# Norms around the two layers of a hybrid decoder step: five tiles in a pipeline instead of one after the other, and the first projection step by halves of the tokens

## Chip, cores and metric

The kernel runs on one core of a Trainium2 chip. The metric is the device time of one execution in microseconds (us), the median of several runs. PE is TensorE, DVE VectorE, ACT ScalarE, POOL GpSimd and SP SyncE, which issues most of the loads. A matmul record's first size is its stationary operand, its second the moving one.

## The reference

```python
for layer in range(2):
    hp, hs = rms_norm(y_prompt, norm_pre), rms_norm(y_sample, norm_pre)
    # layer 0: differential attention over a paged cache; layer 1: retention with a recurrent state
    o = mixer(hp @ w_in, hs @ w_in)            # gate from the same projection
    y = y + rms_norm(o @ w_out, norm_post)

def rms_norm(x, w):
    return x * lax.rsqrt(mean(x * x, axis=-1) + 1e-6) * w
```

There are 512 prompt tokens and 64 sample tokens (T = 576) of 2048 features, all in float32. Before a layer x is normed with weight `norm_pre`; behind it the layer's output y is normed with weight `norm_post` and added to x.

## The kernel before

Projections keep features on the partitions and tokens on the free axis: `XH` and `XL` hold the normed x in two parts (high and low), `WH` and `WL` a weight chunk in two parts. A weight chunk is 512 rows by 256 columns (512 KB), loaded by SP into one of two slots of `WR`, and split by ACT (`WH`, a copy) and DVE (`WL`, a subtraction): stage `split_w`. A step of the projection makes 256 output columns for all 576 tokens: in the input projections it goes over 4 chunks, 32 tiles, and each tile is 6 matmuls, 3 products (high-high, high-low, low-high) for each of two halves of 288 tokens. `Projections.tile` gives out the tiles one by one; behind the third tile of chunk n it puts the split of chunk n+1 and the load of chunk n+3. The attention and retention work is set between the tiles by hand written slot numbers (`attention_pair`, `layer_one`), and the one list of stages that results is run by every engine in order, each engine doing its own part of a stage and waiting on counted semaphores.

The norms need tokens on the partitions. They work on five tiles of tokens (four of 128 and one of 64), and stand in `norm_segment(stage)`, called for stage 0 (before layer 0), 1 (between the layers) and 2 (at the end). The list alternates `y_tile` and `x_tile`:

- `y_tile` (stages 1 and 2): PE transposes a tile of y into the four `low_banks`; ACT squares all 2048 features from there and sums them; DVE scales the sum (L1303), POOL raises it to -0.5 (L1644), DVE multiplies by that and by `wpost` (L1605), and then adds the tile of x that was loaded (L1609).
- `x_tile` (stages 0 and 1): ACT squares the tile of x (L1266), DVE and POOL make the factor as above, ACT multiplies the tile by it, PE transposes it into the four `high_banks`, ACT copies 16 pieces times `wpre` to `XH`, and DVE subtracts to `XL` (L1620).

x and the scaled tile have two buffers each. SP loads a tile of x when its buffer is free. In the last parts of the output projections PE's sums are added to y by DVE (L1346, L1347), two additions for each 128 output columns.

## Time and profile before

| what | us |
|---|---|
| median of 3 runs | 4121.02 (4120.16 to 4127.6) |
| the profiled execution | 4107.18 |
| its span, first to last instruction | 4105.4 |
| first projection matmul, layer 0 | 90.37 |
| last matmul of layer 0, first of layer 1 | 1980.8, 2087.71 |
| last projection matmul of all | 4053.4 |

The time outside the span is 1.8 us. Mean granted clock of TensorE over the span is 0.965 of full speed. The span falls into two long stretches of projections with the mixers' work among them, and three short ones for the norms: before 90.37, from 1980.8 to 2087.71, and behind 4053.4.

### The profile page before, as it was taken

The page shows a single profiled execution, that of the slowest core. Times are in us where ns is not written, and L with a number is a line of the kernel's source. Part 1 is how long each engine was busy: PE and PEld are TensorE (multiplying, and loading weights), DVE is VectorE, ACT ScalarE, POOL GpSimd, SP SyncE. Part 2 cuts the span into 40 slices and gives each one's busy share as a digit, 9 for nine tenths or more (in the row PEclk, how much of TensorE's full clock was granted, in tenths as well). Part 3 has the DMA queues.
Part 4 walks back from the last instruction along what each step waited for, and adds up shares of the span by engine and source line. Part 5 has one row for each costly group of instructions (what it writes and reads, how often), then busy time and mean ns, then how long its engine had stood idle before and what let it go on. Part 6 is the DMA issues. An engine that isn't in the chain of part 4 may idle for free.

```text
span 4105.4 us, 69674 instructions
## 1 busy us (share of the span) xinstructions
PE 3767.5 (92%) x26880; PEld 3289.5 (80%) x26880; DVE 1427.7 (35%) x2278; ACT 1138.2 (28%) x1905; POOL 125.1 (3%) x76
## 2 busy tenths in 40 slices
PE   2998999999999998999579999999999999989996
PEld 2987777777777776776579989898988888879996
DVE  2234333333343334333432423233333334233333
ACT  4233223322332333231332222222222222222221
POOL 0000000200020002002000000000000000000000
PEclk7999999999999998999789999999999999999998
DMA  2355777677767775764323334343424243343323
GB/s 75 106 173 164 233 214 236 190 232 221 238 191 235 218 231 182 228 191 147 113 73 112 125 117 134 111 145 95 154 80 157 79 153 104 133 140 116 106 83 129
DMA packets 466203, 632.41 MB, mean 154 GB/s; under 512 B 39441, under 2 KB 288914, under 8 KB 462738
## 3 DMA queue, kind: packets, MB, share of 16 engines
q1 hardware_dynamic: 401538, 555.71, 43.4%
q10 hardware_dynamic: 64336, 72.24, 5.1%
q8 instruction: 216, 3.54, 0.4%
q14 instruction: 113, 0.93, 0.1%
HBM read 555.61 MB, written 70.65 MB: 153 GB/s over the span
## 4 chain that ended last, share of the span: by engine, by line
PE 53%; DVE 3%; ACT 2%; issue 2%; ACTq 2%; DMA 1%; POOL 1%; SPq 1%; DVEq 0%; POOLq 0%
PE low_banks L832 42%; PE high_banks L832 7%; PE high_banks L835 3%; POOL area L1644 1%; DVE area L1583 1%; ACTq L1245 1%; DVE WL L1328 1%; ACT XH L1055 1%; DVE area L1605 1%; DMA area<-in_cache_v 0%; ACTq L1215 0%; ACT WH L1055 0%; ACTq L1214 0%; PE low_banks L835 0%; ACT area L1055 0%
## 5 line engine op out<-in xcount | busy, mean ns | idle before, releaser
L832 PE MATMUL low_banks<-XH,WH 128*128 128x288 f32 x6656 | 1527.0, 311 | 46.2 <-DVE XL L1333 16.3
L832 PE MATMUL low_banks<-XH,WL 128*128 128x288 f32 x6656 | 1431.9, 297 | 0.0
L832 PE MATMUL low_banks<-XL,WH 128*128 128x288 f32 x6656 | 1428.8, 296 | 0.0
L832 PEld LDWEIGHTS low_banks<-XH,WH 128*128 128x128 f32 x6656 | 1072.5, 191 | 197.0 <-issue 154.5
L832 PEld LDWEIGHTS low_banks<-XH,WL 128*128 128x128 f32 x6656 | 1077.4, 190 | 0.0
L832 PEld LDWEIGHTS low_banks<-XL,WH 128*128 128x128 f32 x6656 | 1077.3, 190 | 0.0
L1328 DVE TENSOR_TENSOR WL<-WR,WH 128x1024 fp32r<-128x1024 f32 x416 | 509.3, 1224 | 965.2 <-ACT WH L1055 964.1
L1055 ACT ACTIVATE WH<-WR 128x1024 fp32r<-128x1024 f32 x416 | 439.9, 1057 | 981.4 <-PE low_banks L832 672.7
L832 PE MATMUL high_banks<-area 128*32 128x512 f32 (+7 forms) x3696 | 670.2, 553 | 45.2 <-issue 17.0
L835 PE MATMUL high_banks<-eye_sb,area 128*128 128x128 f32 (+2 forms) x3048 | 458.8, 287 | 203.2 <-ACT area L1055 150.1
L835 PEld LDWEIGHTS high_banks<-eye_sb,area 128*128 128x128 f32 (+2 forms) x3048 | 362.7, 147 | 346.4 <-issue 182.2
L1055 ACT ACTIVATE area<-high_banks 128x512 f32<-128x512 f32 x480 | 271.9, 569 | 1231.8 <-PE high_banks L835 807.3
L832 PEld LDWEIGHTS high_banks<-area 128*32 128x32 f32 (+4 forms) x3696 | 233.7, 147 | 225.9 <-issue 181.0
L1411 DVE COPY area<-high_banks 128x512 f32<-128x512 f32 x256 | 176.9, 691 | 601.6 <-PE high_banks L835 562.7
L1644 POOL TENSOR_TENSOR area<-area,power 128x1 f32<-128x1 f32 (+2 forms) x72 | 124.9, 1735 | 3970.4 <-DVE area L1303 3970.4
L1112 ACT ACTIVATE area<-low_banks 128x288 f32<-128x288 f32 x192 | 79.0, 411 | 377.8 <-PE low_banks L832 356.6
L1583 DVE SCALAR_TENSOR_TENSOR area<-area,high_banks 128x512 f32<-128x512 f32 x128 | 87.2, 745 | 51.1 <-PE high_banks L832 51.0
L1564 DVE SCALAR_TENSOR_TENSOR area<-area,high_banks 128x512 f32<-128x512 f32 x48 | 35.8, 747 | 166.5 <-PE high_banks L832 164.7
L1346 DVE TENSOR_TENSOR area<-low_banks,area 128x288 f32<-128x288 f32 x80 | 36.6, 458 | 161.0 <-PE low_banks L832 161.0
L1113 ACT ACTIVATE area<-low_banks 128x288 f32<-128x288 f32 x192 | 79.1, 412 | 6.0
L1620 DVE SCALAR_TENSOR_TENSOR XL<-high_banks,wpre,XH 128x128 fp32r<-128x128 f32 (+1 forms) x160 | 40.4, 329 | 72.9 <-ACT XH L1055 72.9
L1596 DVE TENSOR_TENSOR area<-high_banks,area 128x512 f32<-128x512 f32 (+1 forms) x40 | 25.6, 641 | 112.1 <-PE high_banks L835 112.1
(93 smaller groups left out, 901.1 us busy)
## 6 DMA issues: line engine op xcount, KB each, us to landing
area<-in_cache_k SPq DMA_DIRECT2D x512, 256.0 KB, 4.1
area<-in_cache_v SPq DMA_DIRECT2D x512, 256.0 KB, 3.9
WR<-in_w_in_ret SPq DMA_DIRECT2D x192, 512.0 KB, 3.6
WR<-in_w_in_attn SPq DMA_DIRECT2D x128, 512.0 KB, 5.2
out<-area ACTq DMA_DIRECT2D x73, 512.0 KB, 3.9
area<-in_state_ret SPq DMA_DIRECT2D x64, 512.0 KB, 5.5
WR<-in_w_out_ret SPq DMA_DIRECT2D x64, 512.0 KB, 3.4
WR<-in_w_out_attn SPq DMA_DIRECT2D x32, 512.0 KB, 4.9
```

Of the source, the lines that this page charges most:

```text
L832: return nc.tensor.matmul(out, a, b, start=start, stop=stop, skip_group_check=True)
L835: return nc.tensor.matmul(out, a, ident[0:n, 0:n], start=True, stop=True, is_transpose=True, skip_group_check=True)
L1055: return nc.scalar.activation(out, in_, ACT.Copy, scale=scale)
L1112: o.link(nc.scalar.activation(dst[:, 0:HALF], bank[2 * cb][:, 0:HALF], f))
L1113: last = nc.scalar.activation(dst[:, HALF:T], bank[2 * cb + 1][:, 0:HALF], f)
L1245: act.dma_start(st_out[g + b * HEADS], Sin[:, b, :].rearrange("p (e v) -> p e v", e=2)).then_inc(sem["state_out"], 16)
L1328: v.tensor_tensor(WL[:, slot, :, :], WR[:, slot, :, :], WH[:, slot, :, :].bitcast(f32), SUB).then_inc(sem["w_lo"], 1)
L1411: v.tensor_copy(KTs[u % 2][:, :, pp * 128:(pp + 1) * 128], bank[5][:, :].rearrange("p (j s) -> p j s", j=4)).then_inc(sem["drained5"], 1)
L1583: v.scalar_tensor_tensor(out=mine, in0=mine, scalar=hc[:, 388:389], in1=bank[4 + j][:, :], op0=MUL, op1=ADD).then_inc(sem[f"drained{4 + j} ...
L1605: v.scalar_tensor_tensor(out=yv, in0=low[0:R, :, :].rearrange("p a b -> p (a b)"), scalar=n[:, 1:2], in1=wpost[0:R, :], op0=MUL, op1=MUL). ...
L1620: last = v.scalar_tensor_tensor(out=XL[:, j, xc], in0=bank[4 + j // 4][:, (j % 4) * 128:(j % 4) * 128 + R], scalar=wpre[:, stage, j:j + 1] ...
L1644: nc.gpsimd.tensor_tensor(out, a, power[0:R, 0:n], ALU.pow).then_inc(sem[name], 1)
```

## The change

`norm_segment` gives way to `norm_before`, `norm_between` and `norm_last`, which are built by the class `Norm` from smaller stages, and several tiles are under way at once.

- y's squares are no longer summed from the transposed tile. Behind each step of the last part of an output projection ACT squares the 2 x 576 finished values (`y_sq`), and DVE adds them to `yacc` (8 steps for each layer). One group of matmuls with a column of ones then sums over the features for all five tiles (`y_rstd`), and POOL makes all factors in two instructions.
- y's tile comes from PE by ordinary matmuls with a diagonal matrix that holds `norm_post` (`post_diag`), not by transposes; DVE multiplies by the factor and adds x in one pass, in two halves. At the end of the kernel the tiles take the two halves of PSUM in turn.
- x's five tiles have a buffer each. Between the layers and at the end they are loaded, with the row of weights, beside the last part of the output projection. `norm_pre` is now multiplied with tokens on the partitions: tiles 0 and 4 get factor and weights in one pass on DVE; tiles 1 and 3 (and between the layers also 2) get the weights on POOL (`x_weigh`) and the factor on ACT. Copies to `XH` and subtractions to `XL` go by bank (4 of 512 columns).
- The first step of both input projections goes by halves of the tokens: all four chunks for tokens 0 to 287, and the four chunks again, loaded and split a second time, for tokens 288 to 575. Its first half starts when tiles 0 to 2 are there; the transposes of tile 3 stand behind its 10th tile, those of tile 4 behind its 26th.
- At the start SP loads x before the small constants; the exponentials of lambda are made later. The wait before the shared area changes hands (`relay_area`) no longer holds projections and weight loads, which now stand ahead of it.

```diff
 
-    def step(self, w, cols, rows, kts, **kinds):
+    def step(self, w, cols, rows, kts, by_half=False, **kinds):
+        half_chunks = len(rows)
+        if by_half:
+            rows, kts = rows + rows, kts + kts
         count = len(rows) * 2 * CH
         for i in range(count):
...
-                                                     new_x=i == 0, start=chunk == 0 and k == 0, stop=chunk == len(rows) - 1 and k == CH - 1,
+                                                     new_x=i == 0 or by_half and i == count // 2, halves=(chunk // half_chunks,) if by_half else (0, 1),
+                                                     start=chunk % half_chunks == 0 and k == 0, stop=(chunk + 1) % half_chunks == 0 and k == CH - 1,
                                                      full=full)))
...
+    loads = norm_loads(1)
     for n in range(64):
         out += proj.tile()
+        if n % 8 == 3 and loads:
+            out.append(loads.pop(0))
+        if n % 8 == 2 and n > 8:
+            out.append(Stage("y_sq", s=n // 8 - 1))
+    assert not loads
+    out.append(Stage("y_sq", s=7))
     return out
...
+class Norm:
+
+    def __init__(self, stage):
+        self.stage = stage
+        self.y, self.sq, self.weighed, self.scaled, self.tr = {}, {}, {}, {}, {}
+
+    def load(self, t):
+        return [Stage("load_x_tile", t=t, stage=self.stage)]
+
+    def sum_y(self, t):
+        wide = self.stage == 2 and t % 2
+        freed = self.y.get(t - 2 if self.stage == 2 else t - 1)
+        self.y[t] = Stage("y_tr", t=t, stage=self.stage, wide=wide, freed=freed)
+        return [self.y[t]]
+
+    def store(self, t):
+        return [Stage("store_x", t=t, stage=self.stage, after=self.y[t])]
+
+    def square(self, t):
+        self.sq[t] = Stage("x_sq", t=t, stage=self.stage, after=self.y.get(t))
+        return [self.sq[t]]
+
+    def weigh(self, t):
+        self.weighed[t] = Stage("x_weigh", t=t, after=self.y.get(t), freed=self.tr.get(t - 2))
+        return [self.weighed[t]]
+
+    def scale(self, t):
+        weighed = self.weighed.get(t)
+        self.scaled[t] = Stage("x_scale", t=t, by="act" if weighed else "dve", after=self.sq[t], weighed=weighed, freed=self.tr.get(t - 2))
+        return [self.scaled[t]]
+
+    def transpose(self, t):
+        in_low = self.stage == 0 and t == 1
+        freed = [x for u, x in self.tr.items() if not x.a["in_low"]]
+        self.tr[t] = Stage("x_tr", t=t, in_low=in_low, after=self.scaled[t], freed=freed[-1] if freed and not in_low else None)
+        return [self.tr[t]]
+
+    def close(self, proj):
+        out = []
+        for n in range(32):
+            if n == 10:
+                out += self.transpose(3) + self.scale(4)
+            if n == 26:
+                out += self.transpose(4)
+            out += proj.tile()
+        return out
+
+
+def norm_before(proj):
+
+    n = Norm(0)
+    out = n.load(0) + [Stage("load_norm", stage=0)] + n.load(1) + n.load(2) + proj.load(0) + proj.load(1) + n.load(3) + n.load(4)
+    out += [Stage("load_consts")]
+    out += n.square(0) + n.square(1) + n.weigh(1) + n.scale(0) + n.square(2) + n.transpose(0) + n.scale(1) + [Stage("split_w", slot=0)]
+    out += proj.load(2) + n.scale(2) + n.square(3) + n.transpose(1) + n.weigh(3) + n.square(4) + n.transpose(2) + n.scale(3)
+    out += [Stage("lambda_dot")]
+    return out + n.close(proj) + [Stage("lambda_exp")]
+
+
+def norm_between(proj):
+
+    n = Norm(1)
+    out = [Stage("y_rstd")]
+    out += n.sum_y(0) + n.square(0) + n.sum_y(1) + n.weigh(1) + n.scale(0) + n.square(1) + n.store(0)
+    out += n.sum_y(2) + n.transpose(0) + n.weigh(2) + n.square(2) + n.scale(1) + n.store(1)
+    out += n.sum_y(3) + n.transpose(1) + n.weigh(3) + n.square(3) + n.scale(2) + n.store(2)
+    out += n.sum_y(4) + n.transpose(2) + n.square(4) + n.scale(3) + n.store(3) + n.store(4)
+    return out + n.close(proj)
+
+
+def norm_last():
+
+    n = Norm(2)
+    out = [Stage("y_rstd")]
+    for t in range(5):
+        out += n.sum_y(t) + n.store(t)
     return out
+
+
+def norm_loads(stage):
+    out = [Stage("load_x_tile", t=t, stage=stage) for t in range(5)]
+    return [out[0], out[1]] + ([Stage("load_norm", stage=stage)] if stage < 2 else []) + out[2:] + [Stage("post_scale", stage=stage)]
 
 
...
-            proj.step("in0", "qkvg".index(kind) * D + (2 * pair + hh) * 256, rows, xs, kind=kind, hh=hh)
+            proj.step("in0", "qkvg".index(kind) * D + (2 * pair + hh) * 256, rows, xs, by_half=pair == hh == 0 and kind == "q", kind=kind, hh=hh)
...
-            proj.step("in1", col, rows, xs, kind=["q", "k", "v", "v", "g", "g"][s] + "r", hh=s % 2)
+            proj.step("in1", col, rows, xs, by_half=h == s == 0, kind=["q", "k", "v", "v", "g", "g"][s] + "r", hh=s % 2)
...
-                    for half in range(2):
+                    for half in halves:
...
-            def y_tile(g, t, stage):
-                R = TILES[t][1]
-                for n in ("proj0_drained", "proj1_drained", "y_used"):
+            def y_rstd(g):
+                pe.wait_ge(sem["y_acc"], c.before("y_acc"))
+                for n in range(4, 8):
+                    free(n)
+                for t, R in TILES:
+                    last = mm(bank[4][0:R, 2 * t:2 * t + 2], yacc[:, t * 128:t * 128 + R], ones[:, 0:2])
+                last.then_inc(sem["y_sums"], 1)
+
+            def y_tr(g, t, stage, wide, freed):
+                R, to = TILES[t][1], (low, high)[wide]
+                pe.wait_ge(sem["post_ready"], c.before("post_ready"))
+                for n in ("proj0_drained", "proj1_drained"):
                     pe.wait_ge(sem[n], c.before(n))
-                for j in range(KT):
-                    last = tr(bank[j // 4][0:R, (j % 4) * 128:(j % 4) * 128 + 128], yT[:, j, t * 128:t * 128 + R])
-                last.then_inc(sem["y_full"], 1)
-
-            def x_tile(g, t, stage):
-                R = TILES[t][1]
-                pe.wait_ge(sem["x_normed"], c.done("x_normed"))
-                pe.wait_ge(sem["x_lo"], c.before("x_lo"))
-                for j in range(KT):
-                    last = tr(bank[4 + j // 4][:, (j % 4) * 128:(j % 4) * 128 + R], yn[0:R, t % 2, j * 128:(j + 1) * 128], R)
-                last.then_inc(sem["xt_full"], 1)
+                if wide and t == 1:
+                    pe.wait_ge(sem["y_var"], c.before("y_var"))
+                for part in range(2):
+                    if freed is not None:
+                        pe.wait_ge(sem["x_sum"], c.after(freed, "x_sum") - 1 + part)
+                    for j in range(8 * part, 8 * part + 8):
+                        last = mm(to[0:R, j // 4, (j % 4) * 128:(j % 4) * 128 + 128], yT[:, j, t * 128:t * 128 + R], post_diag[:, j, :])
+                    last.then_inc(sem["y_full"], 1)
+
+            def x_tr(g, t, in_low, after, freed):
+                R, to = TILES[t][1], (high, low)[in_low]
+                name = "x_scaled_" + after.a["by"]
+                pe.wait_ge(sem[name], c.after(after, name))
+                if freed is not None:
+                    pe.wait_ge(sem["x_lo"], c.after(freed, "x_lo"))
+                elif not in_low:
+                    pe.wait_ge(sem["y_var"], c.before("y_var"))
+                for b in range(4):
+                    for j in range(4):
+                        last = tr(to[:, b, j * 128:j * 128 + R], xn[0:R, t % 2, (4 * b + j) * 128:(4 * b + j + 1) * 128], R)
+                    last.then_inc(sem["xt_full"], 1)
...
                 R = TILES[t][1]
-                act.wait_ge(sem["y_full"], c.done("y_full"))
-                nc.scalar.activation(njunk[0:R, :], low[0:R, :, :].rearrange("p a b -> p (a b)"), ACT.Square,
...
+            def y_sq(g, s):
+                for n in ("proj0_drained", "proj1_drained", "y_acc"):
+                    act.wait_ge(sem[n], c.before(n))
+                nc.scalar.activation(ysq[:], yT[:, 2 * s:2 * s + 2, :], ACT.Square).then_inc(sem["y_sq"], 1)
...
+            def x_scale(g, t, by, after, weighed, freed):
+                if by == "act":
+                    R = TILES[t][1]
+                    act.wait_ge(sem["x_rstd"], c.after(after, "x_rstd"))
+                    act.wait_ge(sem["x_weighed"], c.after(weighed, "x_weighed"))
...
+            def x_tr(g, t, in_low, after, freed):
+                R, src = TILES[t][1], (high, low)[in_low]
+                for b in range(4):
+                    act.wait_ge(sem["xt_full"], c.done("xt_full") - 3 + b)
+                    copy(XH[:, 4 * b:4 * b + 4, t * 128:t * 128 + R], src[:, b, :].rearrange("p (a t) -> p a t", a=4)[:, :, 0:R]
+                         ).then_inc(sem["x_hi"], 1)
+
...
+                if s:
+                    o.link(v.tensor_tensor(yacc[:], yacc[:], ysq[:, 0, :], ADD))
+                    v.tensor_tensor(yacc[:], yacc[:], ysq[:, 1, :], ADD).then_inc(sem["y_acc"], 1)
+                else:
+                    v.tensor_tensor(yacc[:], ysq[:, 0, :], ysq[:, 1, :], ADD).then_inc(sem["y_acc"], 1)
...
+                    v.scalar_tensor_tensor(out=xt[0:R, t, cols], in0=src[0:R, 2 * part:2 * part + 2, :].rearrange("p a b -> p (a b)"),
+                                           scalar=yss[0:R, 1, t:t + 1], in1=xt[0:R, t, cols], op0=MUL, op1=ADD).then_inc(sem["x_sum"], 1)
...
-                    last = v.scalar_tensor_tensor(out=XL[:, j, xc], in0=bank[4 + j // 4][:, (j % 4) * 128:(j % 4) * 128 + R],
-                                                  scalar=wpre[:, stage, j:j + 1], in1=XH[:, j, xc].bitcast(f32), op0=MUL, op1=SUB)
...
+                    last = v.tensor_tensor(XL[to], src[:, b, :].rearrange("p (a t) -> p a t", a=4)[:, :, 0:R], XH[to].bitcast(f32), SUB)
...
+                nc.gpsimd.tensor_tensor(xn[0:R, t % 2, :], xt[0:R, t, :], norm_row[0:R, :], MUL).then_inc(sem["x_weighed"], 1)
```

DVE's list between the layers began like this before (L1605 and L1609 finish a tile of y, L1620 a tile of x):

```order
L1303 TENSOR_SCALAR area<-area 128x1
L1605 SCALAR_TENSOR_TENSOR area<-low_banks,area 128x2048
L1609 TENSOR_TENSOR area<-area 128x2048
L1303 TENSOR_SCALAR area<-area 128x1
L1605 SCALAR_TENSOR_TENSOR area<-low_banks,area 128x2048
L1609 TENSOR_TENSOR area<-area 128x2048
L1303 TENSOR_SCALAR area<-area 128x1
L1620 SCALAR_TENSOR_TENSOR XL<-high_banks,wpre,XH 128x128 x16
```

It begins like this now (L1724 and L1725 start the factors of y, L1734 is half a tile of y plus x, L1409 an x factor, L1749 the DVE-made x tile, L1757 the subtraction to `XL`):

```order
L1715 TENSOR_TENSOR area<-area 128x576
L1716 TENSOR_TENSOR area<-area 128x576
L1724 TENSOR_SCALAR area<-high_banks 64x1
L1725 TENSOR_SCALAR area<-high_banks 128x4
L1734 SCALAR_TENSOR_TENSOR area<-low_banks,area 128x1024 x2
L1409 TENSOR_SCALAR area<-area 128x1
L1734 SCALAR_TENSOR_TENSOR area<-low_banks,area 128x1024 x2
L1749 SCALAR_TENSOR_TENSOR area<-area 128x2048
L1409 TENSOR_SCALAR area<-area 128x1
L1734 SCALAR_TENSOR_TENSOR area<-low_banks,area 128x1024 x2
L1757 TENSOR_TENSOR XL<-high_banks,XH 128x4x128 x4
```

Three tiles of y now stand ahead of the first subtraction to `XL`, where two did, and a factor (L1409), which waits for ACT's square of the tile before, still stands between one tile of y and the next.

PE's list at that place was this before (L835 are transposes, of y into `low_banks` and of x into `high_banks`):

```order
L835 MATMUL low_banks<-eye_sb,area 128x128 x32
L835 MATMUL high_banks<-eye_sb,area 128x128 x16
L835 MATMUL low_banks<-eye_sb,area 128x128 x16
L835 MATMUL high_banks<-eye_sb,area 128x128 x16
L835 MATMUL low_banks<-eye_sb,area 128x128 x16
L835 MATMUL high_banks<-eye_sb,area 128x128 x16
L835 MATMUL low_banks<-eye_sb,area 64x128 x16
L835 MATMUL high_banks<-eye_sb,area 128x128 x16
L835 MATMUL high_banks<-eye_sb,area 128x64 x16
L832 MATMUL low_banks<-XH,WH 128x288 x2
```

A tile of x and a tile of y took turns. It is this now (L915 from `area` are the products with the diagonal matrix, L918 transposes of x, the last rows the first half step):

```order
L915 MATMUL high_banks<-eye_sb,area 128x2 x4
L915 MATMUL high_banks<-eye_sb,area 64x2
L915 MATMUL low_banks<-area 128x128 x48
L918 MATMUL high_banks<-eye_sb,area 128x128 x16
L915 MATMUL low_banks<-area 128x128 x16
L918 MATMUL high_banks<-eye_sb,area 128x128 x16
L915 MATMUL low_banks<-area 64x128 x16
L918 MATMUL high_banks<-eye_sb,area 128x128 x16
L915 MATMUL low_banks<-XH,WH 128x288
L915 MATMUL low_banks<-XL,WH 128x288
L915 MATMUL low_banks<-XH,WL 128x288
```

Three tiles of y (48 products) stand ahead of the first transposes, and the projection starts behind the transposes of tile 2. In the first half step DVE's list between the layers is now this (`WL` is the split of a chunk):

```order
L1437 TENSOR_TENSOR WL<-WR,WH 128x1024
L1757 TENSOR_TENSOR XL<-high_banks,XH 128x4x128 x4
L1749 SCALAR_TENSOR_TENSOR area<-area 64x2048
L1437 TENSOR_TENSOR WL<-WR,WH 128x1024 x2
L1757 TENSOR_TENSOR XL<-high_banks,XH 128x4x64 x4
L1437 TENSOR_TENSOR WL<-WR,WH 128x1024
```

The splits of chunks 2 and 3 stand behind the subtraction of tile 3 and the scaling of tile 4; before, no norm work stood among splits.

## Rows read from the trace of the kernel before

**Rows 1.** Busy time by stage: PE, PEld, DVE, ACT, POOL, clock, DMA share, GB/s

```profile
22.00:90.40 68.40, 16.45 (x81) 14.89 (x81) 22.05 (x85) 37.70 (x94) 2.19 (x4) 0.67 0.18 62
1940.00:1982.00 42.00, 40.84 (x315) 40.64 (x314) 20.17 (x34) 6.37 (x6) 0.00 (x0) 1.00 0.33 109
1982.00:2085.00 103.00, 30.34 (x160) 28.04 (x158) 42.33 (x88) 48.51 (x98) 5.47 (x10) 0.58 0.26 94
4054.00:4106.00 52.00, 16.22 (x80) 14.08 (x80) 24.42 (x16) 9.84 (x10) 2.74 (x5) 0.62 0.39 142
```

**Rows 2.** Chain that ended last, between the layers: start, us, what

```profile
2000.74 1.79 issue
...
2003.64 2.01 ACT area L1055
...
2005.69 3.69 PE high_banks L835 x16
...
2016.70 2.36 DVE area L1605
...
2019.09 2.30 DVE area L1609
...
2021.44 1.79 issue
```

**Rows 3.** Timeline at the edges of the norm stretches: start, us, what

```profile
117.57 0.41 ACT L1112 ACTIVATE area<-low_banks 128x288 f32<-128x288 f32 x1 [2.35 <-PE low_banks L832]
...
1981.24 0.46 DVE L1347 TENSOR_TENSOR area<-low_banks,area 128x288 f32<-128x288 f32 x1
...
2116.18 0.41 ACT L1112 ACTIVATE area<-low_banks 128x288 f32<-128x288 f32 x1 [2.35 <-PE low_banks L832]
...
4054.02 0.46 DVE L1347 TENSOR_TENSOR area<-low_banks,area 128x288 f32<-128x288 f32 x1
...
4054.57 1.94 PE L835 MATMUL low_banks<-eye_sb,area 128*128 128x128 f32 x16 [1.16 <-issue]
...
4100.57 0.54 ACTq L1284 DMA_DIRECT2D out<-area  x1
```

**Rows 4.** Groups by form on ACT and DVE: busy us, mean ns, idle before

```profile
L1055 ACT ACTIVATE WH<-WR 128x1024 fp32r<-128x1024 f32 x416 | 439.9, 1057 | 981.4 <-PE low_banks L832 672.7 <-issue 191.7 <-DVE area L1596 98.2
...
L1328 DVE TENSOR_TENSOR WL<-WR,WH 128x1024 fp32r<-128x1024 f32 x416 | 509.3, 1224 | 965.2 <-ACT WH L1055 964.1
...
L1055 ACT ACTIVATE area<-high_banks 128x512 f32<-128x512 f32 x416 | 248.0, 598 | 1140.6 <-PE high_banks L835 720.4 <-PE high_banks L832 255.3 <-issue 132.9
...
L1266 ACT ACTIVATE area<-area 128x2048 f32<-128x2048 f32 x8 | 15.3, 1907 | 31.3 <-DVE area L1609 22.8 <-DMA area<-in_x_prompt 8.5
...
L1596 DVE TENSOR_TENSOR area<-high_banks,area 128x512 f32<-128x512 f32 x32 | 22.2, 694 | 75.7 <-PE high_banks L835 75.7
...
L1517 DVE TENSOR_TENSOR area<-area 128x576 f32<-128x576 f32 x16 | 12.1, 758 | 0.6
```

**Rows 5.** Timeline around POOL's longest instruction; and a group by form on POOL

```profile
1903.69 21.66 POOL L1644 TENSOR_TENSOR area<-area,power 128x128 f32<-128x128 f32 x1 [171.27 <-DVE area L1303]
...
1918.32 1.22 DVE L1328 TENSOR_TENSOR WL<-WR,WH 128x1024 fp32r<-128x1024 f32 x1 [0.27 <-ACT WH L1055]
...
L1644 POOL TENSOR_TENSOR area<-area,power 128x4 f32<-128x4 f32 x8 | 8.1, 1017 | 1201.9 <-DVE area L1303 1201.9
```

**Rows 6.** Timeline of PE in an attention pair

```profile
355.75 1.97 PE L832 MATMUL high_banks<-area 128*128 128x256 f32 x8
```

**Rows 7.** Chain in the last output projection

```profile
3834.69 102.68 PE low_banks L832 x768
```

**Rows 8.** Busy time by stage, while three large loads run

```profile
1979.00:1985.00 6.00, 3.58 (x29) 3.14 (x27) 0.92 (x2) 1.14 (x1) 0.00 (x0) 1.00 1.02 415
```

**Rows 9.** Loads: size, median us from issue to landing

```profile
area<-in_x_prompt SPq DMA_DIRECT2D x1, 1024.0 KB, 5.0
...
WR<-in_w_out_ret SPq DMA_DIRECT2D x15, 512.0 KB, 3.4
```

270 lines of the change are left out of this document (138 added, 132 removed).

## The prediction

> **What bounds the kernel now.** I read the busy time by stage first [rows 1]. In the last part of layer 0's output projection PE works 40.84 of 42.00 us while DVE is busy 20.17 and ACT 6.37: PE is the bound, and the two others have room. Between the layers it is the other way: in 103 us PE works 30.34, ACT 48.51 and DVE 42.33, so no engine is the bound. The chain shows why [rows 2]: one tile is finished before the next begins. From the square of one x tile (2000.74) to the next (2021.44) it goes in single file through ACT's scaling 2.01, PE's transposes 3.69, ACT's copies, DVE's two passes over y, 2.36 and 2.30. That is 20.7 us a tile, five times. The start (22.00 to 90.40, PE 16.45 of 68.40) and the end (PE 16.22 of 52.00) are alike [rows 1]. The rest of the kernel is projections at PE's pace: 768 matmuls in 102.68 us, 0.134 each [rows 7], so 0.8 us for a tile of six, 25.7 for a step of 32 tiles and 0.4 for a tile of half the tokens.
>
> The kernel can therefore gain only what the three norm stretches hold, and it gains it one for one, since PE has nothing else to do there. I take each by its far edge. At the start and between the layers the edge is the end of the first projection step, when ACT starts the second drain: 117.57 and 2116.18 [rows 3]. That holds the cost of going by halves too.
>
> **Prices that the rows give.** Split of a chunk: 1.06 on ACT and 1.22 on DVE. A bank copied by ACT 0.60, subtracted by DVE 0.69, so 2.4 and 2.8 for a tile of x where the copies of 16 pieces took over 4. Square of a tile 1.91 and 0.19 for its sum; adding 576 columns 0.76 [rows 4]. ACT's scaling 2.01, and DVE's pass from PSUM 2.36 for 2048 columns, so 1.2 for a half [rows 2]. 16 transposes take 1.94 at full clock and 3.69 at the lower level [rows 2, 3]. Four columns raised to -0.5 on POOL 1.02 [rows 5].
>
> Two prices are not in the trace. One is an ordinary float32 product of 128 columns (the diagonal matrix). The nearest row is 8 records of 256 columns in 1.97 us. The code issues four products there, so a product is two records and takes 0.49, and one of 128 columns about 0.245: 3.9 us for a tile of y at full clock, twice the 1.94 of transposes, and 7.4 at the lower level (3.4 to 5 at full clock as its bounds) [rows 3, 6]. The other is POOL multiplying 2048 columns. From below it is DVE's 2.30 for a pass of that size [rows 2], from above what POOL takes for raising to a power, 21.66 us for 128 columns, 347 for 2048 [rows 5]. A multiplication is far nearer to the first, so I take twice that, 4.6. By the Trainium skill (GPSIMD Engine Reference, section 3.1) this very shape takes 4.5 us there; with it the sum below stays the same. No row here shows it.
>
> **Between the layers.** The last addition to y ends at 1981.70 [rows 3]. The last step's squares cannot hide: ACT 1.2 us (1152 columns), DVE two additions, 1.5, then five short sums on PE, about 1.2, so PE begins on y at about 1986, and the factors are there at 1988. PE then has five tiles of y, 19.5, and three transposes of x, 5.8. It has idled 4 us before them, and after a longer idle a whole burst of 3.69 us ran at the lower level [rows 2], so I count its first 4 us there (+2): 27.4 us of work. ACT has 4 squares, 2 scalings and 3 copies, 20 us, from the first finished tile at 1992.4 on. DVE has more waiting, as each tile of y stands behind the factor of the tile before, and that behind ACT's square: 2.4 + 2.1 + 0.2 and handovers, 5 a tile, with the subtractions in between. Laying all lists out by these prices, ACT ends its copies of tile 2 at 2017, and the projection starts at 2018 (before: 2087.7). The step then takes 25.6 us of matmuls, 2.9 of transposes for tiles 3 and 4, and stalls: chunk 1 is split only behind ACT's scaling of tile 3 (2.2), chunk 2 behind DVE's subtraction of tile 3 and its pass over tile 4 (3.5), and about 1.5 in the rest. It ends at 2053.5 where it ended at 2116.18: 63 less. The five stores of 1 MB that now run beside weight loads, and whatever handovers I missed, take some; I say 59.
>
> **At the start.** SP sends x first, at about 3.5 us. A tile takes 5.0 us to land [rows 9], and behind it they follow at 415 GB/s [rows 8], 2.5 us a megabyte: tile 0 at 8.5, the weights' row, tiles 1 and 2 by 16, tile 4 by 23. From then the lists bind, ACT's above all: five squares 10.5, a scaling 2, a split 1, copies of three tiles 7.2, and some 6 of waiting, mostly for tile 1 and for transposes at the lower clock. The projection starts at about 35.5. The step takes the same 25.6 + 2.9 + 5.5 and ends at 70 against 117.57: 47 less. Loads that land later and a clock that is low longer take a little; I say 45.
>
> **At the end.** The last addition ends at 4054.48 [rows 3]. Squares, additions and sums as above bring PE to y at 4058.6. Five tiles at 3.9, with about 1.5 for the slow start, end at 4079.6; PE is now the bound, as DVE needs only 2.4 a tile. DVE's last half ends at 4080.9, and the last store took 4.83 us to the end of the span (4100.57 to 4105.4 [rows 3]): 4085.7, 19.7 less. I say 18.
>
> **What lies beside other work.** In each layer 8 steps get 1.2 us on ACT and 1.5 on DVE, inside a step of 6.4 us or more, in which DVE is busy by half [rows 1]. Without that cover it would be 22 us a layer. The diagonal matrix is one more pass of 2.3 on DVE, in one step, and can delay an addition there by 1 us. The five loads of x and the row are hidden in the same place, as weights land in 3.4 us [rows 9] and have 10 before they are needed. Four chunks more in each layer cost PE nothing; ACT and DVE split a chunk in 2.3 and a handover, just under the 3.2 that PE spends on a chunk by halves. A slot of `WR` turns in 3.4 + 2.5, just under 6.4. I take 1 us off for all this together.
>
> **Sum.** 59 + 45 + 18 - 1 = 121 us off the profiled execution's 4107.2, 3986. The median of the runs shown lies 13.8 above that execution; taking the same off it gives **4000**.
>
> **Rivals.** (a) *The clock stays low in the norm stretches*, because PE still works in bursts. For it: before, every burst from the second on took about 3.7 us, at the lower level. Against: now PE's work is in one piece for 20 us and more. It would cost 17 us between the layers (start of the projection 2035, end 2070), 16 at the end (37 us for y, not 21), 2 at the start: 4034. Chance 0.07.
> (b) *The half steps are bound by loads and splits.* If chunks land in 5.2 us, not 3.4, or splits queue longer behind the norm work, each of 16 chunks costs about 1 us more: 4016. Chance 0.10.
> (c) *POOL is in the way.* At 9 us a multiplication the three tiles between the layers and the two at the start become the widest link, and the layout gives 7 us more at each: 4014. The Trainium skill (GPSIMD Engine Reference, section 8) says that POOL shares its way to SBUF with DVE instructions that have two SBUF inputs. What the trace has on it: such a DVE pass (`WL`) took 1.22 us in the middle of a POOL instruction of 21.66 [rows 5], as much as its mean [rows 4]; but that POOL work hardly reads, so it says little for a multiplication. Chance 0.08.
> (d) *Slower than before.* This needs POOL's price to be like its power's. The first 4.4 us above 4.6 cost 14 in all, later ones up to 5 for each; from about 30 us a multiplication all 121 is gone, and at 347 the kernel is some 1500 slower. Chance 0.02.
> (e) *The norms were not worth their length*, some other thing being late next (a relay of the area, the constants, layer 1's first tables), so that half of the gain is lost: 4060. Nothing in the rows speaks for it. Chance 0.03.
> The forecast, all prices within their bounds, has 0.70: 3984 to 4018.
>
> **Numbers.** The range that holds 8 in 10 takes (b) and (c) whole and reaches toward (a): 3980 to 4028. A measurement of this kernel can tell about 0.2%, 8 us, from no change. Faster by more than that: 0.97; within it: 0.01; slower: 0.02.
>
> **What the changed profile would show.** The first projection matmul at about 36, its step drained at 70; between the layers, counted from the last addition to y, the projection after 36 us and its step drained after 72 (before 106 and 134.5). The products of three tiles of y in one piece, mostly at the full clock level. L1812 on POOL at 4 to 5 us. No PE gap in the last part of either output projection beyond 1 us. At the end PE's tiles of y 3.9 us apart. It would be wrong if PE is found waiting for POOL or for a chunk of weights for over 10 us, or if the diagonal products take twice their price.

## The result and the profile after

The changed kernel takes 3994.81 us (median of 4 runs, 3990.8 to 3997.85) where the kernel before takes 4120.94 beside it: a ratio of 0.9696, 95% interval 0.9684 to 0.9707. Faster by 126 us, 3.0%. The prediction was 4000, its range 3980 to 4028.

The profiled execution took 3990.8 us (span 3989.0, mean granted clock 0.983) against 4107.18 (0.965). That is 116.4 us less, where the prediction's sum said 121. The medians fell by 126 because the median of before's runs lay 13.8 us above its profiled execution, and that of the changed kernel only 4.0.

I read the change of time by the prediction's own edges. First the timeline of the changed kernel: ACT's second drain of the first projection step (L1216), the last addition to y in each layer (L1456), and the same drain in layer 1.

```profile
71.32 0.41 ACT L1216 ACTIVATE area<-low_banks 128x288 f32<-128x288 f32 x1 [0.74 <-PE low_banks L915]
...
1938.59 0.46 DVE L1456 TENSOR_TENSOR area<-low_banks,area 128x288 f32<-128x288 f32 x1
...
2014.09 0.41 ACT L1216 ACTIVATE area<-low_banks 128x288 f32<-128x288 f32 x1 [0.74 <-PE low_banks L915]
...
3957.67 0.46 DVE L1456 TENSOR_TENSOR area<-low_banks,area 128x288 f32<-128x288 f32 x1
```

With [rows 3] they cut both executions into five stretches:

| stretch | before | after | less | the sum said |
|---|---|---|---|---|
| start, to the drain of the first step | 117.57 | 71.32 | 46.25 | 45 |
| projections and mixer of layer 0, to the last addition | 1864.13 | 1867.73 | -3.6 | -0.5 |
| between the layers, to the drain of layer 1's first step | 134.48 | 75.04 | 59.44 | 59 |
| projections and mixer of layer 1, to the last addition | 1938.30 | 1944.04 | -5.7 | -0.5 |
| end | 50.92 | 30.87 | 20.05 | 18 |

So the three norm stretches gave 125.7 where 122 was forecast, and the two long stretches took back 9.3 where 1 was.

The windows by stage of the changed kernel (columns as in [rows 1]): the first step, the last part of layer 0's output projection, the stretch between the layers, and the end.

```profile
34.00:72.00 38.00, 32.13 (x232) 31.00 (x233) 17.94 (x26) 15.34 (x23) 1.69 (x2) 0.96 0.39 121
...
1890.00:1939.10 49.10, 46.96 (x351) 46.51 (x349) 34.36 (x51) 15.62 (x14) 0.00 (x0) 1.00 0.56 198
...
1939.05:2014.09 75.04, 61.38 (x444) 59.29 (x445) 41.39 (x53) 35.00 (x44) 19.81 (x10) 0.91 0.35 121
...
3958.13:3989.00 30.87, 21.71 (x170) 21.32 (x170) 14.56 (x14) 1.16 (x1) 1.52 (x2) 0.85 0.41 153
```

In the first window PE is idle for 5.9 of 38 us; from the first projection matmul (35.18) to the drain (71.32) it is idle for 4.7. Between the layers it is busy 61 of 75 us at a mean clock of 0.91. At the end it works 21.7 of 30.9, where before it worked 16.2 of 52 [rows 1].

PE's timeline between the layers: the sums over the features, then the products of y's tiles (L915, moving 128x128), x's transposes (L918), and the first projection matmul.

```profile
1942.11 2.14 PE L915 MATMUL high_banks<-eye_sb,area 128*128 128x2 f32 x10 [4.12 <-DVE area L1716]
1944.18 9.70 PE L915 MATMUL low_banks<-area 128*128 128x128 f32 x64
1955.24 3.81 PE L915 MATMUL low_banks<-area 128*128 128x128 f32 x32 [1.36 <-DVE area L1734]
1958.88 1.91 PE L918 MATMUL high_banks<-eye_sb,area 128*128 128x128 f32 x16
1960.63 3.74 PE L915 MATMUL low_banks<-area 128*128 128x128 f32 x32
1965.59 1.97 PE L918 MATMUL high_banks<-eye_sb,area 128*128 128x128 f32 x16 [1.22 <-ACT area L1157]
...
1976.08 0.37 PE L915 MATMUL low_banks<-XH,WH 128*128 128x288 f32 x1 [1.94 <-issue]
```

At the full clock a tile of y is 32 records, two for each product, in 3.7 to 3.8 us: the estimate was 3.9. The first two tiles (x64) took 9.70 together, as the granted clock was at the lower level, 1.2 GHz, from 1942.2 to 1949.0. The ten sums fell into that time too: 2.14 us, forecast 1.2. The projection starts 37.0 us after the last addition (1939.05); forecast 36. At the end the tiles stand 3.6 us apart behind a first one that took 5.25, partly at the lower level (which held from 3959.5 to 3966.3):

```profile
3961.19 2.17 PE L915 MATMUL high_banks<-eye_sb,area 128*128 128x2 f32 x10 [4.12 <-DVE area L1716]
3963.30 5.25 PE L915 MATMUL low_banks<-area 128*128 128x128 f32 x32
3968.38 3.74 PE L915 MATMUL high_banks<-area 128*128 128x128 f32 x32
3971.95 3.74 PE L915 MATMUL low_banks<-area 128*128 128x128 f32 x32
```

The chain between the layers (start, length, what) runs through POOL once, for tile 1's weights:

```profile
1956.36 4.51 POOL area L1812
1960.87 2.06 issue
1962.93 0.58 POOL area L1779
1963.53 2.01 ACT area L1157
```

The chain gives POOL's multiplication 4.51 us, as much as it takes alone, and shows 2.06 more as "issue"; the timeline has it all as one instruction of 6.62 us. It began 0.16 us behind a pass of DVE with two operands in SBUF (L1749), and such a pass takes 2.34:

```profile
1956.20 2.34 DVE L1749 SCALAR_TENSOR_TENSOR area<-area 128x2048 f32<-128x2048 f32 x1
...
1956.36 6.62 POOL L1812 TENSOR_TENSOR area<-area 128x2048 f32<-128x2048 f32 x1 [1.88 <-DVE area L1734]
...
1963.45 4.59 POOL L1812 TENSOR_TENSOR area<-area 128x2048 f32<-128x2048 f32 x1
```

At the start the same thing met POOL's power (a factor raised to -0.5), 2.62 us at 16.08 where it takes 0.55 at 12.50, beside DVE's pass that began at 15.94.

Of the signs that the prediction named, POOL's 6.62 is outside its 4 to 5 us, and the longest gap of PE in the last eight steps of layer 0's output projection is 1.03 us against its 1; in layer 1's there is none.

### The profile page after: what moved, and what is told of

Read it like the earlier page. It is cut to its first block, busy times and chain, and to the rows that moved or that the text cites. A ratio compares the mean times of both kernels' runs of the same rounds, so it can differ in the third digit from the quotient of the medians.

```text
span 3989.0 us, 70024 instructions
## 1 busy us (share of the span) xinstructions
PE 3778.5 (95%) x27060; PEld 3298.9 (83%) x27060; DVE 1436.0 (36%) x2197; ACT 1111.8 (28%) x1784; POOL 149.3 (4%) x75
## 4 chain that ended last, share of the span: by engine, by line
PE 54%; DVE 3%; ACTq 2%; ACT 2%; DMA 1%; issue 1%; SPq 1%; POOL 1%; DVEq 0%
PE low_banks L915 43%; PE high_banks L915 8%; PE high_banks L918 2%; DVE WL L1437 1%; DVE area L1692 1%; DMA area<-in_cache_v 1%; ACTq L1349 1%; POOL area L1779 1%; ACT WH L1157 1%; ACTq L1318 1%; SPq L850 1%; ACTq L1319 1%; SPq L851 0%; DVE XL L1442 0%; DMA area<-in_cache_k 0%
## 5 line engine op out<-in xcount | busy, mean ns | idle before, releaser
L915 PE MATMUL low_banks<-XH,WH 128*128 128x288 f32 x6656 | 1541.4, 312 | 51.3 <-DVE WL L1437 23.5
L915 PE MATMUL low_banks<-XH,WL 128*128 128x288 f32 x6656 | 1442.9, 297 | 0.0
L915 PE MATMUL low_banks<-XL,WH 128*128 128x288 f32 x6656 | 1440.9, 297 | 0.0
L915 PEld LDWEIGHTS low_banks<-XH,WH 128*128 128x128 f32 x6656 | 1077.5, 191 | 205.7 <-issue 151.6
L915 PEld LDWEIGHTS low_banks<-XL,WH 128*128 128x128 f32 x6656 | 1082.8, 190 | 0.0
L915 PEld LDWEIGHTS low_banks<-XH,WL 128*128 128x128 f32 x6656 | 1081.7, 190 | 0.0
L1437 DVE TENSOR_TENSOR WL<-WR,WH 128x1024 fp32r<-128x1024 f32 x424 | 519.0, 1224 | 945.0 <-ACT WH L1157 939.8
L915 PE MATMUL high_banks<-area 128*32 128x512 f32 (+5 forms) x3760 | 681.9, 550 | 48.0 <-issue 16.2
L918 PEld LDWEIGHTS high_banks<-eye_sb,area 128*128 128x128 f32 (+2 forms) x3032 | 347.7, 143 | 232.7 <-issue 178.0
L918 PE MATMUL high_banks<-eye_sb,area 128*128 128x128 f32 (+2 forms) x3032 | 442.0, 280 | 91.5 <-DVE area L1749 19.5
L915 PEld LDWEIGHTS high_banks<-area 128*32 128x32 f32 (+2 forms) x3760 | 242.3, 148 | 230.3 <-issue 182.3
L1779 POOL TENSOR_TENSOR area<-area,power 128x1 f32<-128x1 f32 (+3 forms) x66 | 124.7, 1890 | 3813.9 <-DVE area L1409 3337.5
L1216 ACT ACTIVATE area<-low_banks 128x288 f32<-128x288 f32 x192 | 78.9, 411 | 370.3 <-PE low_banks L915 349.4
L1442 DVE TENSOR_TENSOR XL<-XL,XH 128x576 fp32r<-128x576 f32 (+1 forms) x48 | 36.1, 752 | 45.0 <-ACT XH L1157 43.7
```

Of the source, the lines that this page charges most:

```text
L915: return nc.tensor.matmul(out, a, b, start=start, stop=stop, skip_group_check=True)
L918: return nc.tensor.matmul(out, a, ident[0:n, 0:n], start=True, stop=True, is_transpose=True, skip_group_check=True)
L1216: o.link(nc.scalar.activation(dst[:, 0:HALF], bank[2 * cb][:, 0:HALF], f))
L1437: v.tensor_tensor(WL[:, slot, :, :], WR[:, slot, :, :], WH[:, slot, :, :].bitcast(f32), SUB).then_inc(sem["w_lo"], 1)
L1779: nc.gpsimd.tensor_tensor(out, a, power[0:R, 0:n], ALU.pow).then_inc(sem[name], 1)
```

## Experiments

Each experiment is read by the same five stretches, since single medians move by several us. All of them:

| kernel | median, us | start | layer 0 | between | layer 1 | end |
|---|---|---|---|---|---|---|
| before (first profile) | 4121 | 117.57 | 1864.13 | 134.48 | 1938.30 | 50.92 |
| before_again | one run, 4115.1 | 117.80 | 1865.43 | 134.22 | 1945.03 | 50.82 |
| changed (first profile) | 3994.8 | 71.32 | 1867.73 | 75.04 | 1944.04 | 30.87 |
| after_again | 3996.3 | 71.47 | 1873.55 | 75.60 | 1942.16 | 31.72 |
| nohalf | 4007.5 | 75.30 | 1870.88 | 77.97 | 1948.24 | 30.91 |
| squares_last | 4038.9 | 71.42 | 1873.28 | 94.40 | 1950.30 | 51.00 |
| nopool | 3997.1 | 69.27 | 1873.14 | 75.81 | 1944.15 | 31.23 |
| splits_first | 3989.5 | 65.83 | 1874.94 | 70.67 | 1946.05 | 30.91 |
| post_first | 3996.0 | 71.64 | 1869.82 | 74.39 | 1946.43 | 31.02 |
| combo | 3996.6 | 66.07 | 1874.95 | 72.91 | 1949.47 | 31.40 |
| pool_zero | 3989.2 | 66.91 | 1874.92 | 68.74 | 1948.20 | 31.33 |
| start_dve | 3985.7 | 66.38 | 1867.63 | 70.15 | 1948.93 | 30.91 |
| dve_twice | one run, 4020.8 | 77.21 | 1872.07 | 85.49 | 1952.79 | 31.44 |

**The kernel before, once more (before_again).** No edit.

> The kernel before, unchanged, for a second profile. The first profiled execution took 4107.2 us where the timed runs took 4120 to 4128. If the 14 us belong to the kernel's timed runs, this profile is again near 4107 and the timed run near 4121. If they are a difference from one execution to the next, the two should lie within 5 us of each other here. The three norm stretches keep their length: first step drained at 117.6, from the last addition of layer 0 to the drain of layer 1's first step 134.5, from the last addition of all to the end 50.9.

It took 4115.11 us, and 4107.18 in the first profile. The runs beside it took 4119.94 to 4131.86, with a median of 4120.95. So 8 of the 14 us are a difference from one execution to the next; but both profiled executions lie below every run that stood beside them. The norm stretches repeat within 0.3 us. The projections do not: layer 1's stretch is 6.7 us longer in one execution than in the other, with the same kernel.

**No halves (nohalf).** Both first steps go over all tokens at once, and tiles 3 and 4 are finished before them.

```diff
     def close(self, proj):
-        out = []
-        for n in range(32):
-            if n == 10:
-                out += self.transpose(3) + self.scale(4)
-            if n == 26:
-                out += self.transpose(4)
-            out += proj.tile()
-        return out
+        return self.transpose(3) + self.scale(4) + self.transpose(4)
...
-            proj.step("in0", ..., by_half=pair == hh == 0 and kind == "q", kind=kind, hh=hh)
+            proj.step("in0", ..., kind=kind, hh=hh)
```

> The changed kernel, but both first projection steps go over all tokens at once, behind the transposes of all five tiles; no chunk is loaded or split twice. Theory: going by halves hides most of tiles 3 and 4 but pays for stalls on the splits (7.6 us in the first step); laid out by the prices of the rows, undoing it lengthens the start by 2.3 us and the stretch between the layers by 2.5, so about 5 us in all, 1.001 of the changed kernel's time. Rival: the halves carry much of the gain, since they start the projection 11 us earlier at each place; then the kernel loses 15 to 22 us. Rival on the other side: stalls cost more than they hide, and this is faster by some us.

4007.49 us (4000.7 to 4010.8, ratio 0.9719, interval 0.9705 to 0.9733), 11 to 13 us behind the changed kernel. The stretches give 4.0 at the start and 2.9 between the layers, 6.9 in all, nearer to the theory's 5 than to the rival's 15; the rest lies in the long stretches, whose scatter is as large. So in the norm stretches going by halves is worth about 7 us; the other 4 to 6 of the medians' difference are not explained. The first projection matmul came at 47.41 instead of 35.18: the halves gain 12 us of start and give 8 back, in a second round of splits and in stalls.

**Squares behind the projection (squares_last).** All eight `y_sq` of a layer stand behind the last projection step.

```diff
-        if n % 8 == 2 and n > 8:
-            out.append(Stage("y_sq", s=n // 8 - 1))
-    out.append(Stage("y_sq", s=7))
+    out += [Stage("y_sq", s=s) for s in range(8)]
```

> The changed kernel, but all eight squares of y and their additions stand behind the last projection of each layer, not beside its last part. Theory: each square and its additions is one link of about 2.9 us (1.17 on ACT, 2 times 0.76 on DVE, handovers), seven more of them at each place cost 2 x 20 = 40 us, less what the last parts of the output projections give back (they lost 3.3 us in layer 0 and some of 5.7 in layer 1): net 33 to 38 us slower than the changed kernel. Rival: the losses in the last parts come from the loads of x and the pass that builds the diagonal matrix, not from the squares; then nothing is given back and it is 40 slower, and from the seventh step on the steps of layer 0 still show a stall.

4038.94 us (ratio 0.9793, interval 0.9778 to 0.9808), 44 us over the changed kernel's 3994.8. The two norm stretches are 19.4 and 20.1 longer, 39.5 in all: the rival's 40, not the theory's net 33 to 38, as the long stretches as a whole gave nothing back (the last steps of layer 0 gave 1.25, see post_first). The rival's stall in the later steps is not there either. A step of squares costs 2.93 us when nothing covers it, because ACT and DVE wait for each other: the next square needs the buffer that DVE is adding. Two steps' rows from DVE's timeline:

```profile
1951.22 0.76 DVE L1712 TENSOR_TENSOR area<-area 128x576 f32<-128x576 f32 x1 [1.38 <-ACT area L1357]
1952.01 0.76 DVE L1713 TENSOR_TENSOR area<-area 128x576 f32<-128x576 f32 x1
1954.15 0.76 DVE L1712 TENSOR_TENSOR area<-area 128x576 f32<-128x576 f32 x1 [1.38 <-ACT area L1357]
```

So 40 of the 126 us come from the cover alone. What the cover costs is read from the last 49.1 us of layer 0's stretch. In the changed kernel PE is busy for 46.96 of them (above), and for 47.03 in after_again. Here are before, squares_last, and post_first (below), in this order:

```profile
1932.60:1981.70 49.10, 48.04 (x368) 47.81 (x367) 23.23 (x39) 7.43 (x7) 0.00 (x0) 1.00 0.29 95
```

```profile
1895.60:1944.70 49.10, 48.04 (x361) 47.81 (x359) 25.41 (x40) 7.44 (x7) 0.00 (x0) 1.00 0.58 204
```

```profile
1892.36:1941.46 49.10, 48.04 (x361) 47.81 (x359) 33.86 (x53) 15.61 (x14) 0.00 (x0) 1.00 0.58 203
```

The last has the squares beside the projection and PE is as busy as without them. The squares alone cost nothing there.

**No POOL (nopool).** `weigh` is removed everywhere; DVE gives each tile factor and weights in its one pass.

```diff
-    out += n.square(0) + n.square(1) + n.weigh(1) + n.scale(0) + n.square(2) + ...
+    out += n.square(0) + n.square(1) + n.scale(0) + n.square(2) + ...
```

> The changed kernel without multiplications on POOL: all five tiles get factor and weights in one DVE pass of 2.35 us. In the trace POOL's multiplication took 4.5 us, and 6.6 where a DVE pass with two SBUF inputs ran beside it. Theory: ACT's list is the long one between the layers, and it gets 2 us a tile shorter while DVE's gets 2.35 longer; the layout gives 0 at the start and +2 us between the layers, so 0 to 3 us slower in all (within 0.1%). Rival: POOL's link on the chain (4.5 + 2.1 between the layers) was the late one, and this is 4 to 7 us faster.

3997.06 us (ratio 0.9699, interval 0.9684 to 0.9713): not to be told from the changed kernel. The start is 2.05 us shorter (the layout had 0), the stretch between the layers 0.77 longer (it had 2). POOL's help is worth nothing in sum, and taking its longer multiplication off the chain did not bring the rival's 4 to 7 us.

**The changed kernel, once more (after_again).**

> The changed kernel once more, unedited, beside its three variants, so that they are compared on one chip. Theory: the norm stretches are fixed by lists and prices and repeat within 0.5 us (first step drained at 71.3, 75.0 us from the last addition of layer 0 to the drain of layer 1's first step, 30.9 us from the last addition of all to the end), while the two stretches of projections between them (1867.7 and 1944.0) move by several us with the number of short falls of the granted clock. Rival: the stretches of projections are as fixed as the norms (within 0.5 us), and the 9 us by which they were longer than before is a cost of the change.

3996.3 us (3992.68 to 4001.52). The start and the stretch between the layers repeat within 0.6 us, the end within 0.9; layer 0's stretch is 5.8 us longer than in the first profile, layer 1's 1.9 shorter. The theory stands, though the norm stretches move by a little more than the 0.5 us it gave them. What moves the long ones can be seen in windows over the whole stretch of layer 1, of before and of before_again:

```profile
2116.18:4054.48 1938.30, 1886.38 (x13472) 1751.33 (x13470) 649.19 (x811) 472.46 (x714) 12.51 (x16) 0.99 0.36 118
```

```profile
2117.45:4062.48 1945.03, 1892.78 (x13472) 1757.79 (x13470) 649.14 (x811) 472.11 (x714) 12.50 (x16) 0.99 0.36 118
```

The same 13472 matmuls keep PE busy 6.4 us longer, and DVE and ACT do not change. One place where the two part, first in before, then in before_again:

```profile
3680.00:3700.00 20.00, 15.39 (x113) 14.01 (x112) 10.55 (x13) 6.55 (x11) 0.00 (x0) 1.00 0.68 230
```

```profile
3682.00:3702.00 20.00, 15.39 (x93) 14.02 (x92) 9.86 (x13) 5.13 (x8) 0.00 (x0) 0.83 0.63 211
```

PE has the same two gaps in both, of 1.7 and 2.9 us. In the first its clock stays at 1.00 (2.4 GHz), in the second the mean is 0.83, which is 6.8 us at half of that, and 20 matmuls fewer fit. The execution is 2.7 us later behind it. Going matmul by matmul, the larger falls that stand in only one of the two profiles make 5.3 of the 6.7 us. The pace of matmuls at the full clock (last section) takes 2.0 off ahead of the last eight steps and adds 2.6 in them. The lost clock (length times 1 less the granted clock) in layer 1's stretch is 17.1 us in the first profile and 23.9 in the second, 6.8 more for a stretch that is 6.7 longer. In layer 0's stretch it is 35.8 in both profiles of before; in the changed kernel it is 35.8 and 42.7, for 1867.7 and 1873.6.

**Splits ahead of the norm (splits_first).** The tile of the projection is given out before the transposes and the scaling, so that the chunk's split stands ahead of them in ACT's and DVE's lists.

```diff
         for n in range(32):
+            out += proj.tile()
             if n == 10:
                 out += self.transpose(3) + self.scale(4)
             if n == 26:
                 out += self.transpose(4)
-            out += proj.tile()
```

> In the two first steps the split of chunks 2 and 4 now stands ahead of the transposes and the scaling of tiles 3 and 4 in the lists of ACT and DVE. Theory: the waits of PE for WL in these steps (4.7 us at the start, 5.1 between the layers) are mostly for splits that stand behind norm work; without it each place ends 3.8 us earlier by my layout, so drained at 67.5 and 71.2 us after the last addition, 7.5 us in all. Rival: PE's waits are for weight chunks still on their way (WR took 3.3 to 5.6 us to land and ACT waited 6.9 us for it); then the two places gain under 1 us each and ACT's waits for WR grow by as much as PE's shrink.

3989.45 us (3985.67 to 4003.75, ratio 0.9679, interval 0.9663 to 0.9696), 7 us under after_again. The start is 5.6 us shorter than in after_again and the stretch between the layers 4.9. The waits around the first step (us in total, times, longest) in the changed kernel and here:

```profile
ACT WH L1157 <- DMA WR<-in_w_in_attn: 6.9, 3, 3.3
PEld low_banks L915 <- DVE WL L1437: 5.6, 4, 3.3
PE low_banks L915 <- DVE WL L1437: 4.7, 4, 3.0
```

```profile
ACT WH L1157 <- DMA WR<-in_w_in_attn: 2.5, 1, 2.5
PEld low_banks L915 <- issue: 1.9, 1, 1.9
PEld low_banks L915 <- DVE WL L1437: 1.6, 2, 1.1
```

The rival is out: ACT's wait for the weight chunks shrank with PE's waits, it did not grow. The chunks had been late because the split before them was: a slot of `WR` is loaded again only once its chunk is split. The norm stretches gave 10 where the layout had 7.5; the intervals of the totals overlap.

**The diagonal matrix earlier (post_first).**

```diff
-    return [out[0], out[1]] + ... + out[2:] + [Stage("post_scale", stage=stage)]
+    return [Stage("post_scale", stage=stage), out[0], out[1]] + ... + out[2:]
```

> The pass that makes the diagonal matrix moves from behind the last load of x to ahead of the first, some steps earlier in the last part of both output projections. Theory: that 2.29 us pass held up an addition on DVE and with it PE, 1.5 to 3.5 us once in each layer, wherever it stands beside a full DVE; placed beside the first step it costs less, so 1 to 2 us in layer 0's stretch of projections. Rival: the loss in that stretch is falls of the granted clock, and the time stays within 1 us of the changed kernel once the clock's share is taken out.

3996.03 us (3993.61 to 3999.17, ratio 0.9691): level with after_again. PE is busy for 48.04 of the last 49.1 us, where it was 46.96 and 47.03 in the changed kernel. The pass alone does not cost that 1 us: in squares_last it stands where it did, without the squares, and PE is busy for 48.04 too. It costs where it stands directly behind a step's squares and the addition to y waits for both, as in the changed kernel:

```profile
1927.27 0.76 DVE L1716 TENSOR_TENSOR area<-area 128x576 f32<-128x576 f32 x1
1928.06 2.29 DVE L1708 TENSOR_TENSOR area<-eye_sb,post 128x2048 f32<-128x2048 f32 x1
1930.27 0.45 DVE L1455 TENSOR_TENSOR area<-low_banks,area 128x288 f32<-128x288 f32 x1
```

The time from the last addition of the first of these eight steps to that of the eighth says the same: 46.06 and 46.04 us in the two profiles of the changed kernel, 44.80 in post_first, squares_last and before_again, 43.68 in before. So 2.4 of layer 0's 3.6 us arose here: 1.25 by pass and squares together, and 1.1 by the pace of PE, which was faster in that one profile of before (last section). The expectation's 1 to 2 us came (1.25), but not from the pass wherever it stands.

**Both edits, and the squares of x behind the next tile of y (combo).**

```diff
-    out += n.sum_y(0) + n.square(0) + n.sum_y(1) + n.weigh(1) + n.scale(0) + n.square(1) + n.store(0)
+    out += n.sum_y(0) + n.sum_y(1) + n.square(0) + n.weigh(1) + n.scale(0) + n.store(0)
...
```

> Both edits together, and between the layers the square of an x tile stands behind the sums of the next tile of y, so that DVE's pass over y no longer waits for ACT's square. Theory: 3.8 us at the start, 5.2 between the layers (3.8 and 1.4), 1 for the diagonal pass: 10 us under the changed kernel on the same chip, about 3985. Rival: weight chunks on their way bind (see splits_first), and only 2 to 3 us come.

3996.57 us (3987.08 to 3997.19, ratio 0.9684, interval 0.9671 to 0.9697): the expected 3985 is missed. The new order lost 2.2 us between the layers against splits_first (72.91 and 70.67) where it should have gained 1.4. One instruction shows why, in times from the last addition 15.25 and 15.31:

```profile
1956.27 4.51 POOL L1812 TENSOR_TENSOR area<-area 128x2048 f32<-128x2048 f32 x1
...
1956.33 6.59 DVE L1749 SCALAR_TENSOR_TENSOR area<-area 128x2048 f32<-128x2048 f32 x1 [0.67 <-POOL area L1779]
```

Here POOL started first, by 0.06 us, and it was DVE that stood: 6.59 us for a pass of 2.34. In the changed kernel DVE was first by 0.16 us and POOL stood. That this clash is what turned the gain into a loss is tested by pool_zero below.

**DVE's pass twice (dve_twice).** L1749 is written twice in a row, with the same result.

> DVE makes its pass with factor and weights (two operands in SBUF, 2048 columns, 2.34 us) twice in a row, with the same result. Theory: of POOL's work and such a pass of DVE, whichever starts first runs at its own pace and the other stands still until it is done. Then POOL's multiplication of tile 1 between the layers, which starts 0.16 us behind DVE's pass and took 6.62 us where it takes 4.51 alone, takes 8.9 now, and POOL's power for tile 1 at the start (2.62 where 0.55 is usual) about 5.0; DVE's two passes take 2.34 each. Rival: the two share the way to SBUF and both are slowed, POOL by a fixed start-up price; then POOL stays near 6.6 and 2.6, or DVE's passes take over 2.5.

The numbers that the theory gave (8.9 and 5.0) were wrong; those written down for the rival came (POOL near 6.6 and 2.6, a DVE pass over 2.5). Taken as numbers the experiment spoke for the rival. What speaks against it is when each instruction ends. POOL and DVE between the layers:

```profile
1966.56 6.54 POOL L1814 TENSOR_TENSOR area<-area 128x2048 f32<-128x2048 f32 x1 [1.88 <-DVE area L1734]
...
1966.40 2.34 DVE L1749 SCALAR_TENSOR_TENSOR area<-area 128x2048 f32<-128x2048 f32 x1
1968.78 6.47 DVE L1751 SCALAR_TENSOR_TENSOR area<-area 128x2048 f32<-128x2048 f32 x1
```

DVE's first pass ran at its own pace, and POOL ended 4.36 us behind it (1968.74 to 1973.10), about what it takes alone. DVE's second pass ended 2.15 us behind POOL (1975.25), about what it takes alone. So one stood until the other was done, and neither was slowed while it ran: a shared way would have slowed DVE's first pass. The theory had only missed that POOL gets its turn between the two passes. At the start the turns look different for POOL's power:

```profile
16.01 2.62 POOL L1781 TENSOR_TENSOR area<-area,power 128x1 f32<-128x1 f32 x1 [2.98 <-DVE area L1409]
18.61 6.39 POOL L1814 TENSOR_TENSOR area<-area 128x2048 f32<-128x2048 f32 x1
...
15.87 2.35 DVE L1749 SCALAR_TENSOR_TENSOR area<-area 128x2048 f32<-128x2048 f32 x1
18.26 2.35 DVE L1751 SCALAR_TENSOR_TENSOR area<-area 128x2048 f32<-128x2048 f32 x1
```

The power stood behind DVE's first pass, but its own last 0.4 us did not hold DVE's second pass, which took its usual 2.35. The multiplication then stood until that pass was over (20.61) and ended 4.39 us later. Clashes and added passes cost 10 us between the layers.

**Tile 0's weights on POOL too (pool_zero).** On top of combo.

```diff
-    out += n.sum_y(0) + n.sum_y(1) + n.square(0) + ...
+    out += n.sum_y(0) + n.weigh(0) + n.sum_y(1) + n.square(0) + ...
```

> The combined kernel, but between the layers tile 0 too gets its weights on POOL and its factor on ACT, so that DVE has no pass with two operands in SBUF there before the last tile. Theory: in the combined kernel DVE's pass started 0.06 us behind POOL's multiplication and took 6.59 us for 2.34, which turned a gain of 1.4 into a loss of 2.2; without the clash the stretch from the last addition of layer 0 to the drain of layer 1's first step takes 68.9 to 70 us (the layout gives 68.9) where splits_first had 70.7 and the combined kernel 72.9. The whole is 3 us under the combined kernel, and level with splits_first. Rival: ACT, which gets one scaling more, becomes the bound: over 72.

The stretch takes 68.74 us (expected 68.9 to 70), 4.2 under combo: with no such pass of DVE there before the last tile, the new order gives what the layout said. The whole: 3989.15 us (3981.12 to 3991.83), ratio 0.9671, interval 0.9656 to 0.9685; 7 us under combo where 3 were expected, with layer 0's stretch at its long value (1874.92) in the profile.

**Splits first, and no POOL at the start (start_dve).**

```diff
-    out += n.square(0) + n.square(1) + n.weigh(1) + n.scale(0) + ...
+    out += n.square(0) + n.square(1) + n.scale(0) + ...
```

> splits_first with POOL taken out of the norm at the start alone (all five tiles get factor and weights in DVE's one pass there). Theory: without POOL the start was 2.05 us shorter than in the changed kernel (drained at 69.27, not 71.32), between the layers 0.8 longer; with both edits the step at the start is drained at about 64 (splits_first 65.8), and the whole is 2 us under splits_first. Rival: with the splits moved ahead, DVE has no room left for two passes more, and the start stays at 65.8 or above.

The rival held: the start takes 66.38 us, not 64 (splits_first 65.83). So the 2 us that nopool had gained do not add to what the splits' new place gains; that both removed the same stalls is likely but not shown. The whole was 3985.69 us (3980.24 to 3991.97), ratio 0.9669, interval 0.9654 to 0.9684, the lowest of all; the profile puts that on layer 0's stretch, 1867.63 against 1874.94 in splits_first, with 34.1 us of lost clock against 41.0, and not on the edit.

start_dve, pool_zero and splits_first are all some 0.13 to 0.23% under the changed kernel (0.9692, interval 0.9679 to 0.9705, in after_again). Their intervals touch it, so the total alone does not prove it; the start and the stretch between the layers, which repeat within 0.6 us, do: 71.5 and 75.6 for the changed kernel, 66.9 and 68.7 for pool_zero.

## Why the prediction was right, point by point

The mechanism was right in each of its three parts, and each part was sized within about 2 us. Of the 126 us two runs test some 47 by taking an edit out: the cover of the squares (40) and the halves (7). The rest, several tiles under way at once, is read from the stretches and timelines; no run takes it out alone.

- *Between the layers, 59.* Measured 59.44. The projection began after 37.0 us (said 36), its step was drained after 75.04 (said 72, with 4 us held back in the sum for handovers). Up to the first matmul two terms were too small, the sums (2.14, not 1.2) and POOL's multiplication (held for 2.1 by DVE's pass), and others too large, as the projection came only 0.7 later than laid out. The step itself took 38.0 where the layout had 35.5. Its waits were not the reason, as PE stood idle for 5.1 us in it where 7.2 of stalls were laid out. The layout had PE at the full clock throughout; the granted clock fell to its lower level twice (1976.3 to 1979.7 and 1990.0 to 1993.4), a mean of 0.91 and so 3.4 us lost:

```profile
1976.08:2014.09 38.01, 32.91 (x226) 31.82 (x227) 17.27 (x22) 14.82 (x21) 0.54 (x1) 0.91 0.47 144
```
- *Start, 45.* Measured 46.25. First projection matmul at 35.18 (said 36), drained at 71.32 (said 70). In the step, too, the clock fell once (47.8 to 51.2, 1.7 us lost), and PE stood idle for 4.7 us where 5.5 of stalls were laid out.
- *End, 18.* Measured 20.05; the layout before rounding down had 19.7. The products set the pace there, at 3.6 us a tile, and DVE's last halves followed them.
- *Prices that no row had.* A float32 product of 128 columns is two records, 3.7 to 3.8 us a tile (said 3.9). POOL's multiplication of 2048 columns is 4.51 to 4.59 where it ran alone (said 4.6), beside the 4.5 that the Trainium skill gives for an addition of this size (GPSIMD Engine Reference, section 3.1). Both choices, the double of the nearest row, held.
- *What lies beside other work, -1.* This is the term that was mis-sized: the two long stretches were 9.3 us longer in the profiles. Of its own items the diagonal matrix, behind the squares of one step, cost 1.25 us in layer 0 where 1 was given, and the squares alone nothing (squares_last, post_first). Another 1.1 in layer 0 and 2.6 in layer 1 are the faster pace that before had in its last steps in that one profile. In layer 1 the rest is within what before_again differs from before, 6.7 us. Layer 0 is less clear: all eleven profiles of the changed kernel and its variants have that stretch at 1867.6 to 1875.0 us, and both of before at 1864.1 and 1865.4. Their lost clock there is 34.1 to 47.8 us, before 35.8 both times. Windows over the whole stretch say how much is left, in the changed kernel:

```profile
71.32:1939.05 1867.73, 1763.07 (x12704) 1424.50 (x12702) 687.64 (x1260) 560.50 (x973) 101.45 (x36) 0.98 0.66 203
...
2014.09:3958.13 1944.04, 1889.94 (x13472) 1753.68 (x13470) 661.33 (x825) 480.24 (x721) 12.50 (x16) 0.99 0.36 119
```

PE stands idle 104.7 and 54.1 us there; before it was 101.9 (1864.13 less 1762.24) and 51.9 (1938.30 less 1886.38), and 101.4 and 52.3 in before_again. So 2.8 and 2.2 us are more idle time, and 0.8 and 3.6 more busy time for the same matmuls, which is clock and pace. Over all variants layer 0's idle time scatters from 100.7 to 107.8, so I do not split the 2 to 3 us a layer further. Whether timed runs lose anything in the long stretches is open: the medians fell by 126, as much as the three norm stretches gave alone (125.7).
- *From the profile to the median.* The prediction took 121 off the median of before, as if the 13.8 us between that and the profiled execution would stay. They did not (4.0 after, 0 in after_again, 5.8 in before_again). An error of 4.6 in the sum and one of 10 here had opposite signs, and the total was off by 5. That it was not off by 10 is luck. Why timed runs of before lie above its profiled ones is open; nothing in a profile can show it.

The rivals. (a) *The clock stays low* is out: between the layers the granted clock was 0.91 where it had been 0.64, and all of y's tiles but the first ran at 3.7 to 3.8 us, the full level. (b) *Half steps bound by loads and splits* did not come as an extra: the layout had 5.5 and 7.2 us of stalls in these steps, and PE stood idle for 4.7 and 5.1. Their main cause was the order of ACT's and DVE's lists, not the loads, as splits_first shows, which got 10 us of them back. (c) *POOL in the way*: its multiplication took 4.5, but one was stretched to 6.6. The prediction set the rule of the Trainium skill (GPSIMD Engine Reference, section 8: POOL and DVE share their way to SBUF where a DVE instruction reads two SBUF operands) against a POOL instruction of 21.66 us and found that it said little. That very row held a sign of it, for it began 0.16 us behind a split, and a power of the same size with no split just ahead of it took 0.91 less:

```profile
773.06 20.75 POOL L1644 TENSOR_TENSOR area<-area,power 128x128 f32<-128x128 f32 x1 [10.07 <-DVE area L1303]
775.88 1.23 DVE L1328 TENSOR_TENSOR WL<-WR,WH 128x1024 fp32r<-128x1024 f32 x1 [2.90 <-ACT WH L1055]
...
1903.53 1.22 DVE L1328 TENSOR_TENSOR WL<-WR,WH 128x1024 fp32r<-128x1024 f32 x1
```

The runs bear the rule out, and not as a slowdown: one stands until the other's instruction ends. The clash held POOL for 2.1 us on the chain of the changed kernel and DVE for 4.3 in combo, of which pool_zero gave 4.2 back. What the 2.1 cost in the end is not shown: nopool, without them, was no shorter between the layers. (d) and (e) found nothing.

## What to carry to other kernels

Where the profile shows several engines all half idle and a chain that passes through each in turn for one tile after another, the time is that of the chain, and laying out every engine's list by hand with prices from rows sized this pipeline of tiles to within about 2 us a stretch. Then look at what stands ahead of what in each engine's list: chunks' splits behind two norm stages cost more here (10 us) than going by halves gained (7). And before a difference of a few us is put down to an edit, cut the execution at fixed edges and profile the same kernel twice: stretches of handovers repeated within a microsecond, long matmul stretches did not within six.

## What the runs showed of the hardware

- *POOL and DVE take turns.* A POOL multiplication and a DVE pass, both with two SBUF operands, exclude each other, whole instructions at a time, first come first: 6.62 for 4.51 (POOL behind DVE by 0.16 us), 6.59 for 2.34 (DVE behind POOL by 0.06 us), and alternating in dve_twice. DVE passes that read one operand from PSUM do not take part: L1734 and L1757 ran at 1.24 and 0.62 us each while multiplications ran beside them.
- *POOL's power waits for DVE, but does not hold it.* It took 2.62 us for 0.55 behind a DVE pass, and 21.66 for 20.75 behind a split of 1.22. But a split in the middle of the 20.75 took its usual 1.23, and DVE's second pass in dve_twice its usual 2.35 beside the end of a power.
- *PE's clock falls or stays on the same gaps.* Behind the same two gaps of 1.7 and 2.9 us the granted clock stayed at 1.00 in one execution of before and fell to half for 6.8 us in the other. The two long stretches of before have 21 and 22 falls, which lose 1.7 to 8.5 us of clock each. Of the 22 in before_again, 18 stand at the same work as in before, and 4 are its own. Of those in only one profile, the ones that lose 1.7 us made the execution 1.2 to 1.5 us longer, the ones that lose 3.4 made it 2.4 to 2.7 longer.
- *The pace of matmuls at the full clock has two values.* Four steps in a row of the last part of layer 0's output projection took 24.96 us in one profile of before and 25.60 in the other, four steps of layer 1's 49.92 and 51.20, and in the changed kernel's two profiles 51.20 and 49.92. The granted clock reads 1.00 in all of them. What sets it I did not find.
